# Latent attention: pieces of the first half's values between transposes, and the next round's first scores ahead of the last values

## The reference

```python
q = (rms_norm(c_q, q_norm) @ w_q_up).reshape(b, s, MLA_HEADS, MLA_QK_DIM)
kv = (rms_norm(c_kv, kv_norm) @ w_kv_up).reshape(b, s, MLA_HEADS, MLA_NOPE_DIM + MLA_V_DIM)
...
sc = jnp.einsum("bqhd,bkhd->bhqk", qn, k_nope) + jnp.einsum("bqhd,bkd->bhqk", qr, k_rope)
sc = sc.astype(jnp.float32) * scale
p = jax.nn.softmax(jnp.where(causal, sc, -jnp.inf), axis=-1)
return jnp.einsum("bhqk,bkhd->bqhd", p.astype(v.dtype), v)
```

## Time and profile before

| what | value |
|---|---|
| median of 3 runs | 2382.09 us (2378.76 to 2388.35) |
| the profiled execution | 2379.21 us |
| its span | 2377.4 us |
| its mean granted TensorE clock | 0.985 of 2.4 GHz |
| TensorE matmul busy | 2263.8 us, 95% |
| VectorE, ScalarE, GpSimd busy | 1174.1, 717.6, 1018.6 us |
| first score matmul, last value matmul of the attention | 302.0, 480.6 us |

### The profile page before, as it was taken

One profiled execution on the slowest core, in us unless ns is written; L12 is line 12 of the kernel. 1 busy time (PEld: TensorE's weight loads), 2 busy tenths in 40 slices (PEclk: granted clock), 3 DMA queues, 4 the chain that ended last, 5 costly groups with the idle time before them and its releaser, 6 DMA issues.

```text
span 2377.4 us, 27401 instructions
## 1 busy us (share of the span) xinstructions
PE 2263.8 (95%) x9894; PEld 1745.2 (73%) x9894; DVE 1174.1 (49%) x1223; ACT 717.6 (30%) x1119; POOL 1018.6 (43%) x821
## 2 busy tenths in 40 slices
PE   6999999899899999999999979999999999999998
PEld 5777755577688888888887667777766776788877
DVE  5864355536654343333344877666555444511123
ACT  4343255533311111111112344455434323200112
POOL 2533410166644444444445543233245452444475
PEclk8999999999999999999999989999999999999999
DMA  5111100032211111111112320001001111111153
GB/s 194 54 36 36 36 10 10 34 117 80 64 52 53 44 50 47 51 46 46 51 45 64 116 80 27 27 27 31 31 27 36 44 37 34 37 53 44 53 159 116
DMA packets 34031, 130.61 MB, mean 55 GB/s; under 512 B 4132, under 2 KB 4516, under 8 KB 33196
## 3 DMA queue, kind: packets, MB, share of 16 engines
q1 hardware_dynamic: 30960, 111.39, 14.8%
q10 hardware_dynamic: 3004, 18.30, 2.1%
HBM read 117.04 MB, written 12.58 MB: 55 GB/s over the span
## 4 chain that ended last, share of the span: by engine, by line
PE 83%; DVE 8%; ACT 4%; issue 3%; DMA 1%; POOL 1%; SPq 0%; ACTq 0%; DVEq 0%; POOLq 0%
PE PG L655 13%; PE PG L660 13%; PE PG L661 13%; PE PG L1181 5%; PE PG L1187 5%; PE PG L1186 5%; PE PG L1002 2%; PE PO L1029 1%; PE PO L1331 1%; PE PO L1252 1%; PE PT L1016 1%; PE PG L1322 1%; PE PG L708 1%; PE PG L713 1%; PE PG L714 1%
## 5 line engine op out<-in xcount | busy, mean ns | idle before, releaser
L550 POOL TENSOR_TENSOR WH<-WR,zero 128x512 fp32r<-128x512 f32 x380 | 414.7, 1091 | 1248.3 <-PE PG L655 681.1
L553 POOL TENSOR_TENSOR WL<-WR,WH 128x512 fp32r<-128x512 f32 x380 | 540.0, 1421 | 29.8
L655 PE MATMUL PG<-HH,WH 128*128 128x512 f32 x1136 | 450.5, 397 | 2.4 <-issue 1.5
L660 PE MATMUL PG<-HL,WH 128*128 128x512 f32 x1136 | 443.9, 391 | 0.0
L661 PE MATMUL PG<-HH,WL 128*128 128x512 f32 x1136 | 443.8, 391 | 0.0
L655 PEld LDWEIGHTS PG<-HH,WH 128*128 128x128 f32 x1136 | 214.0, 188 | 52.5 <-issue 6.1
L660 PEld LDWEIGHTS PG<-HL,WH 128*128 128x128 f32 x1136 | 214.2, 189 | 46.0 <-issue 2.2
L661 PEld LDWEIGHTS PG<-HH,WL 128*128 128x128 f32 x1136 | 214.1, 188 | 45.1
L1181 PE MATMUL PG<-HH,WH 128*128 128x512 f32 x544 | 231.4, 425 | 4.9 <-ACTq L1990 2.7
L1187 PE MATMUL PG<-HH,WL 128*128 128x512 f32 x544 | 214.4, 394 | 0.0
L1186 PE MATMUL PG<-HL,WH 128*128 128x512 f32 x544 | 213.9, 393 | 0.0
(11 more groups left out here) (516 smaller groups left out, 4180.2 us busy)
## 6 DMA issues: line engine op xcount, KB each, us to landing
WR<-weights SPq DMA_DIRECT2D x196, 512.0 KB, 3.5
RAW<-x SPq DMA_DIRECT2D x8, 512.0 KB, 7.5
x_spill<-X ACTq DMA_DIRECT2D x1, 4096.0 KB, 12.7
X<-x_spill ACTq DMA_DIRECT2D x1, 4096.0 KB, 12.1
x_spill<-X ACTq DMA_DIRECT2D x4, 1024.0 KB, 5.2
X<-x_spill ACTq DMA_DIRECT2D x8, 512.0 KB, 3.9
y<-RAW SPq DMA_DIRECT2D x7, 512.0 KB, 4.7
POSI<-positions ACTq DMA_DIRECT2D x1, 512.0 KB, 15.8
```

Source lines behind the costliest of these rows:

```text
L550: pool.tensor_tensor(WH[:, slot, part], WR[:, slot, part], zero[:, :].to_broadcast([P, HALF]), ALU.add).then_inc(w_hi, 1)
L553: pool.tensor_tensor(WL[:, slot, part], WR[:, slot, part], WH[:, slot, part].bitcast(F32), ALU.subtract).then_inc(w_split, 1)
L655: m = pe.matmul(out[:, cut], WH[:, slot, w], hi[:, cut], start=n == 0, stop=False)
L660: pe.matmul(out[:, cut], WH[:, slot, w], lo[:, cut], start=False, stop=False)
```

## The change

- The values of half 0 are four pieces, `value(0, j)` for j = 0 to 3, each a matmul for both heads. The piece j = 0 stands ahead of the transposes of t = 4. The pieces j = 1, 2, 3 stand between the transposes of the first and the second head of t = 4, 5, 6. Each piece increments `pv_half` once; the values of half 1 do so once at their end, five increments in a round.
- Half 0's operands lie in blocks 4 to 7 of `PTB` (the copies of t = 0 to 3 go there). The copies of t = 4 to 7 for keys 0 to 3 go to blocks 0 to 3 without a wait; those for keys 4 to 7 go to blocks 4 to 7 and wait for the piece that read the block last.
- TensorE issues the next round's two scores of t = 0 (with their wait for the rotated keys, `krot_done`) ahead of the round's last values. ScalarE's exponentials of these stand ahead of its copy of `PO`. VectorE's stream stays as it is.

```diff
@@ TensorE
-                def values(h):
-                    pe.wait_ge(t_free, i * 24 + (8 if h == 0 else 24))
-                    if h == 0:
+                def value(h, j):
+                    a = max(0, j * P - h * HALF)
+                    for hh in range(2):
+                        at = (2 * i + hh) * 64
+                        m = pe.matmul(PO[hh * 64:(hh + 1) * 64, h, a:HALF], VP[:, j, at:at + 64],
+                                      PTB[:, hh, j + 4 * (1 - h), a:HALF], start=j == 0, stop=j == 4 * h + 3)
+                    return m
+
+                def early_values(j):
+                    if j == 0:
+                        pe.wait_ge(t_free, i * 24 + 8)
                         primed(pe, att_free, i)
                         pe.wait_ge(n_done, NDONE["ssd"])
...
+                    value(0, j).then_inc(pv_half, 1)
+
+                def late_values():
+                    pe.wait_ge(t_free, i * 24 + 24)
+                    for j in range(TT):
+                        m = value(1, j)
+                    m.then_inc(pv_half, 1)
+
...
                     if t == 4:
-                        values(0)
+                        early_values(0)
+                    transposes(t, 0)
+                    if 4 <= t < 7:
+                        early_values(t - 3)
+                    transposes(t, 1)
+                if i < 3:
+                    pe.wait_ge(krot_done, 2 * i + 4)
                     for hh in range(2):
-                        transposes(t, hh)
-                values(1)
+                        scores(0, hh, i + 1)
+                late_values()
@@ ScalarE
-                        if t % 4 == 0 and q == 0:
-                            primed(act, pv_half, i * 4 + (1 + hh if t else 0))
-                        m = min(4, t + 1 - 4 * q)
-                        act.activation(PTB[:, hh, 4 * q:4 * q + m, (t % 4) * P:(t % 4 + 1) * P],
+                        if t == 0:
+                            primed(act, pv_half, 5 * i)
+                        if q == 1:
+                            primed(act, pv_half, 5 * i + t - 3)
+                        m, at = min(4, t + 1 - 4 * q), 0 if t >= 4 and q == 0 else 4
+                        act.activation(PTB[:, hh, at:at + m, (t % 4) * P:(t % 4 + 1) * P],
...
-                primed(act, pv_half, 4 * i + 4)
+                if i < 3:
+                    exp(0, 0, i + 1)
+                    exp(0, 1, i + 1)
+                primed(act, pv_half, 5 * i + 5)
```

More of the change, by code:

```diff
@@ L995, in _, with scores @@
             for i in range(MLA_HEADS // 2):
-                def scores(t, hh):
+                def scores(t, hh, i=i):
                     n = mla_group(i, t, hh)
@@ L1018, in transposes @@
                         m.then_inc(t_ready, 1)
-                def values(h):
-                    pe.wait_ge(t_free, i * 24 + (8 if h == 0 else 24))
-                    if h == 0:
+                def value(h, j):
[8 more added lines that the diff above has]
+                        pe.wait_ge(t_free, i * 24 + 8)
                         primed(pe, att_free, i)
                         pe.wait_ge(n_done, NDONE["ssd"])
[L1025 to L1034, removed]
+                    value(0, j).then_inc(pv_half, 1)
[4 more added lines that the diff above has]
+                    m.then_inc(pv_half, 1)
                 if i == 0:
+                    pe.wait_ge(krot_done, 2)
                     Groups("kv").wait_free(pe, 6)
                     Groups("kv").wait_free(pe, 7)
-                for hh in range(2):
-                    scores(0, hh)
+                    for hh in range(2):
+                        scores(0, hh)
                 for t in range(TT):
@@ L1732, in _, with exp @@
             for i in range(MLA_HEADS // 2):
-                def exp(t, hh):
+                def exp(t, hh, i=i):
                     n = mla_group(i, t, hh)
@@ L1746, in evacuate_pair @@
                         act.wait_ge(t_ready, i * 24 + (n + 1))
-                        if t % 4 == 0 and q == 0:
-                            primed(act, pv_half, i * 4 + (1 + hh if t else 0))
-                        m = min(4, t + 1 - 4 * q)
-                        act.activation(PTB[:, hh, 4 * q:4 * q + m, (t % 4) * P:(t % 4 + 1) * P],
+                        if t == 0:
[4 more added lines that the diff above has]
+                        act.activation(PTB[:, hh, at:at + m, (t % 4) * P:(t % 4 + 1) * P],
                                        PT[:, n % 2, 0:m * P].rearrange("p (b n) -> p b n", b=m),
                                        ACT.Copy).then_inc(t_free, 1)
-                exp(0, 0)
-                exp(0, 1)
+                if i == 0:
+                    exp(0, 0)
+                    exp(0, 1)
                 for t in range(TT):
```

## The result

| what | before | after |
|---|---|---|
| median of the runs | 2382.09 us (2378.76 to 2388.35, 7 runs) | 2370.82 us (2369.89 to 2373.90, 7 runs) |
| the profiled execution | 2379.21 us | 2369.89 us |
| its span | 2377.4 us | 2368.1 us |
| the attention, from the scaling of round 1's second queries to the last copy of PO | 302.22 to 480.96, 178.74 us | 301.32 to 469.54, 168.22 us |

The ratio is 0.995, with a 95% interval of 0.9939 to 0.9962. The change is faster, and the interval holds the 0.5% that the prediction named as a bound, so on which side of it the gain lies isn't told. The forecast was 2371.3 us, 10.8 us less; the medians give 11.3 us less. The better measure for single steps is the length of the attention in the table, whose two ends are starts in the trace. It fell by 10.52 us.

What follows compares the result with a forecast made beforehand. It took the attention rounds to be bound by TensorE, with holes of a tenth to a fifth. 5.15 + 4.83 + 0.83 = 10.8 us off 2379.21 gives 2368.4, plus 2.9 to the median 2371.3 us; range 2364.5 to 2378.

Steps and rivals of the forecast that it cites:

- The holes: Between two heads' transposes at t = 4, 5, 6: three value pieces hide there, 1.29 us a round, 5.15 us in all.
- margin of 0.05 us at t = 4: Transposes, piece and switch take 1.38 us of the 1.43 us between first and second transposes, so the piece fits.
- The stands: TensorE's waits for PTB copies ahead of transposes should fall from 11.7 us to about 6.5.
- The boundary: Between rounds: scores(2, 0) come 1.91 us behind the values' end, not 3.52; gain 1.61 us, three times, 4.83 us.
- margin of 0.09 us behind the copy of PO: At a round's boundary ScalarE finishes the PO copy 0.09 us before the exponential of scores(1, 0) is due.
- Round 4: At its start: GpSimd's weight splits pass under the values, slowed normalisations are covered; gain 0.83 us, 0 if they run over.
- The concurrent heads: Value matmuls of both heads: by the skill's rule a piece costs half, gain about 2.6 us, not 5.15; rule not used.
- rival 1: Holes close less, margins at t = 4 and behind the PO copy fail: gain 8.2 us, or 7.4 (2374.7 us); chance 0.16.
- Rival 4: The copy chain sets the pace mid-round, only the boundaries gain: 5.7 us, 2376.4 us; chance 0.08.
- Rival 3: Granted clock falls to 1.2 GHz inside the attention, in every round: slower, 2391 us at 5 us a round; chance 0.04.
- Rival 2: Clock restarts behind the attention come out better: gain 13.5 us, 2368.6 us; chance 0.12.

Runs made afterwards that it cites:

- e1: Changed kernel with the next round's first scores back behind the last values and ScalarE copying PO ahead of their exponentials; attention 173.86 us, ratio to before 0.9969.
- e5: Changed kernel, but ScalarE copies PO ahead of the exponentials of the next round's first scores; attention 174.01 us.
- e10: Kernel before, but in round 4 the weight slots are released by the scores of t = 5, not t = 0; attention 177.93 us.
- e2: Changed kernel with the first half's four pieces in one block ahead of the transposes of t = 4; attention 175.53 us, ratio to before 0.9971.
- e7: Changed kernel with each piece one hole later and the first half's operands back in blocks 0 to 3 of PTB; attention 181.60 us.
- e9: The same kernel as e2, profiled once more; attention 173.12 us.
- e4: Changed kernel with each piece one hole later, pieces 0 to 3 at t = 4 to 7; attention 166.89 us, ratio to before 0.9945.
- e3: Changed kernel with the first half's operands back in blocks 0 to 3 of PTB; attention 168.79 us.
- e8: Against e4, piece 3 stands beside piece 2 in the hole of t = 6, none at t = 7; attention 165.53 us, ratio to before 0.9940.
- e11: Against e8, the second head's next query projections stand between the two heads' transposes of t = 7; attention 164.62 us, ratio to before 0.9939.

## Why the prediction held, step by step

- **The holes.** The chain from the scores of t + 1 over maximum, exponential and copy set the second transposes, and the pieces moved nothing at t = 5 and 6: 1.67 and 1.70 us from first to second transposes, with and without piece. The prediction gave 1.29 us a round. In the trace it is 1.23: the margin of 0.05 us at t = 4 wasn't there, the interval grew from 1.43 to 1.49, and TensorE doesn't stand in it. Less 0.57 for the transposes and 0.64 for the piece, 0.28 us are left for the switches; the sum had 0.17, with bounds of 0 and 0.34. Four rounds make 4.9 us, e1 4.88, the prediction had 5.15.
- **The stands.** They fell by 6.5 us and not by 5.2 as I wrote (I gave 6.5 us left, 5.2 are left). A piece also fills the hole with the switches on both sides of it, which I had counted in the fit and forgotten here. The gain is the matmul time moved, not the fall of the stands.
- **The boundary.** 1.61 us predicted, 3.52 - 1.91 = 1.61 measured at the first. The margin of 0.09 us behind the copy of PO held. In rounds 2 and 3 the copies of PO are 45.35 - 42.53 = 2.82 us closer, against 1.61 + 1.23 = 2.84. I named ScalarE's release of the score tile as the chain; e5 shows that without ScalarE's new order none of it comes.
- **Round 4.** 0.83 us predicted. What is left of the 10.52 is 10.52 - 4 x 1.23 - 3 x 1.61 = 0.77 us. That the splits caused the loss was read from rows; e10 bears it out with 0.81 us.
- **The concurrent heads.** The rule of the Trainium skill that the prediction cites ("TensorE: Matmul & The Clock Gate", Part 3 on packing), by which a piece would cost half, doesn't hold for these matmuls here either: piece 0 alone takes 1.01 us for 2048 columns of passes, 0.85 us one after another at 2.4 GHz.
- **Rivals.** Of rival 1 there is the 0.06 us at t = 4 and no more. Rival 4 falls with e1, where the pieces gain without the boundary. Rival 3, the clock in the attention, did not come in the changed kernel: it is 1.00 over the rounds. But a fall is nearer than I thought. In three of the thirteen profiled executions the half clock appeared, in round 4 of e2 and of e7 and in round 3 of e5, each time behind a stand of 1.2 to 1.5 us, and in e9, with the same program as e2, it did not. Each was one fall in one round; by the lengths it cost 1.0 us in e5, 2.4 in e2 and, as an estimate from 14.7 - 10.8, 3.9 in e7; the falls in every round that rival 3 needs were not seen. Rival 2 went the other way in the profiled execution. Its restart behind the attention:

```profile
473.00:476.00 3.00, 2.57 (x6) 2.11 (x7) 3.00 (x5) 3.00 (x7) 1.64 (x2) 0.50 0.00 0
476.00:479.00 3.00, 3.00 (x9) 2.28 (x9) 3.00 (x4) 3.00 (x6) 1.57 (x1) 0.54 0.09 22
```

  was slow until about 479 us, over 5 us, where the one of before was slow for some 2.7 us from 484.86. At the first projection the profile was 484.86 - 473.43 = 11.43 us ahead (0.90 of it from ahead of the attention), at ScalarE's first copy of projected rows to RAW 497.19 - 486.92 = 10.27 us, and at the end 9.3 us. The last 1.0 us is a balance of later gains and losses. The largest loss lies at the end of the feed-forward part: the lead over the kernel before was 9.66 us at a clearing of SUM on VectorE (1284.49 before, 1274.83 after) and 8.29 us at its next instruction (1286.65 and 1278.36). The granted clock had fallen there, and before it had not:

```profile
1282.00:1284.00 2.00, 2.00 (x11) 1.65 (x10) 0.90 (x1) 1.06 (x1) 0.00 (x0) 1.00 0.26 107
```

  is the kernel before, and the changed one at the same work, about 10 us earlier, has:

```profile
1272.00:1274.00 2.00, 2.00 (x6) 1.52 (x6) 0.88 (x2) 1.06 (x1) 0.00 (x0) 0.50 0.48 186
```

- **The sum.** 10.8 us against 10.52 in the attention; the terms' errors are -0.23, 0 and -0.06 us. The median gained 11.3 us. The 0.8 us between isn't settled: the runs of one kernel spread by more than that.
- **The hit of 2371.3.** That it came within 0.5 us of the median is luck. The profiled execution was forecast at 2368.4 and took 2369.89, 1.5 us more; then 2.9 us were added as the distance from the profiled execution to the median, and it was 0.9. The two errors cancel. What the prediction had right beyond luck is the attention, 10.8 against 10.52 us. The lower end of its range, 2364.5, doesn't follow from its terms either: 2378.76 - 13.5 is 2365.3.

## What to carry to other kernels

When an engine waits between two pieces of work, find where the chain that ends the wait starts; work put behind that start is free up to the length of the hole, and counts with its switches. Look at the order of the engine that releases the buffers as well: at this boundary the new order of TensorE was worth nothing, but for the slots of round 4, until ScalarE's matched it. Where another place for an operand takes a wait away, it pays in full only if the wait was late: 14.7 us between e4 and e7, part of it the clock's, and 0.57 us between the changed kernel and e3, where the wait was always over.

## What the runs showed of the hardware

- The spread of the runs goes largely with TensorE's clock. Of 20 runs of the kernel before on one chip, the eight of 2378.66 to 2380.14 us had a mean granted clock of 0.985 to 0.987, and the two of over 2386 us had 0.981. It isn't the clock alone: on another chip a run of 2385.26 us had 0.986.
- The clock can fall to its lower level inside the attention, behind stands of 1.24 us (e2), 1.30 us (e7) and 1.52 us (e5). At the same place of round 4 a stand of 1.24 us in the kernel before and in e9, and one of 1.35 us in e4, e8 and e11, left it at 1.00, and so did stands of 1.51 and 1.52 us at the other two boundaries of e5. What decides isn't shown.
- A wait that is already satisfied costs ScalarE about 0.05 us where it stands ahead of the first copy (0.36 against 0.31 us from readout to copy); on a chain that ends a stall this reaches the sum. Ahead of the second copy of a pair, where the changed kernel has it, it doesn't show: the pair takes 0.87 us in both.
- GpSimd's splits slowed VectorE's normalisations by up to 1.07 us (0.29 to 1.29, 0.62 to 1.69 in e10), and its reductions from PSUM not at all (0.96 and 0.94 us beside splits, 0.96 and 0.95 without).
